# Expert layer of a two-block model: which weight slot an overflow tile uses, and in which order the weight loads are issued

## The reference, cut to what matters

```
# 32 experts, every token is sent to 2 of them: 512 (token, expert) rows
expert_id, weights = route(h)                # top-1 group of 8 experts, then top-2 inside it
ys[row] = (silu(x_row @ w_gate[e]) * (x_row @ w_up[e])) @ w_down[e]    # 2048 -> 256 -> 2048, float32
m[token] = sum over its two rows of weight * ys[row]
x = x + gate2 * m
```

## Time and profile before

| | |
|---|---|
| median of three runs | 2995.3 us |
| the profiled execution's own time | 2994.91 us |
| its span | 2993.1 us |
| mean granted TensorE clock | 0.89 of full |
| TensorE matmul busy | 2464.2 us (82%) |
| expert stage, first to last use of expert weights | 2343.4 to 2963.8 us of the span |
| bytes moved by DMA over the span | 610.12 MB |

### The profile page before, as it was taken

One profiled execution on the slowest core, in us unless ns is written; L12 is line 12 of the kernel. 1 busy time (PEld: TensorE's weight loads), 2 busy tenths in 40 slices (PEclk: granted clock), 3 DMA queues, 4 the chain that ended last, 5 costly groups with the idle time before them and its releaser, 6 DMA issues. The chain is left out here.

```text
span 2993.1 us, 42486 instructions
## 1 busy us (share of the span) xinstructions
PE 2464.2 (82%) x18072; PEld 1904.0 (64%) x18072; DVE 1146.7 (38%) x1421; ACT 810.1 (27%) x995; POOL 4.1 (0%) x8
## 2 busy tenths in 40 slices
PE   5997769977998898799999999959465767777774
PEld 5995549934786765699989989848334423333331
DVE  4752445544534301454554555544422211111112
ACT  3443223221113311444344344344201110111110
POOL 0000000000000000000000000000000000000000
PEclk8997889988977999899999999979786788899887
DMA  4447443565214510455555554334204597888886
GB/s 185 199 169 310 196 170 135 202 275 225 114 52 168 203 73 40 169 183 183 197 183 183 197 184 182 141 135 177 104 0 184 242 410 320 357 359 361 351 357 277
DMA packets 58490, 610.12 MB, mean 204 GB/s; under 512 B 5970, under 2 KB 6354, under 8 KB 13266
## 3 DMA queue, kind: packets, MB, share of 16 engines
q1 hardware_dynamic: 51410, 590.90, 49.9%
q10 hardware_dynamic: 6336, 12.58, 1.1%
q0 software_dynamic: 576, 4.19, 0.4%
HBM read 674.76 MB, written 14.68 MB: 230 GB/s over the span
## 5 line engine op out<-in xcount | busy, mean ns | idle before, releaser
L1883 DVE TENSOR_TENSOR ffn_w_lo<-ffn_raw,ffn_w_hi 128x2048 fp32r<-128x2048 f32 x128 | 293.1, 2291 | 234.5 <-ACT ffn_w_hi L1876 234.5
L2587 PE MATMUL psum<-moe_raw,moe_x_t 128*32 128x512 f32 x1536 | 240.0, 754 | 152.7 <-DMA moe_raw<-in_moe 151.2
L1876 ACT ACTIVATE ffn_w_hi<-ffn_raw 128x2048 fp32r<-128x2048 f32 x128 | 244.9, 1914 | 360.6 <-PE psum L1915 355.8
L1913 PE MATMUL psum<-u_hi,ffn_w_hi 128*128 128x256 f32 x1024 | 291.1, 284 | 15.1 <-DVE ffn_w_lo L1883 14.0
L1914 PE MATMUL psum<-u_lo,ffn_w_hi 128*128 128x256 f32 x1024 | 290.8, 284 | 0.0
L1915 PE MATMUL psum<-u_hi,ffn_w_lo 128*128 128x256 f32 x1024 | 290.8, 284 | 0.0
L2587 PEld LDWEIGHTS psum<-moe_raw,moe_x_t 128*32 128x32 f32 x1536 | 50.8, 126 | 273.9 <-issue 227.9
L1913 PEld LDWEIGHTS psum<-u_hi,ffn_w_hi 128*128 128x128 f32 x1024 | 197.7, 193 | 16.0 <-DVE ffn_w_lo L1883 14.2
L1913 PE MATMUL psum<-ffn_w_hi,ffn_hid_hi 128*128 128x512 f32 x512 | 199.4, 389 | 0.0
L1914 PE MATMUL psum<-ffn_w_lo,ffn_hid_hi 128*128 128x512 f32 x512 | 199.4, 389 | 0.0
L1915 PE MATMUL psum<-ffn_w_hi,ffn_hid_lo 128*128 128x512 f32 x512 | 199.2, 389 | 0.0
(11 more groups left out here) (538 smaller groups left out, 4492.2 us busy)
## 6 DMA issues: line engine op xcount, KB each, us to landing
moe_raw<-in_moe SPq DMA_DIRECT2D x144, 2048.0 KB
ring<-in_stream SPq DMA_DIRECT2D x107, 2048.0 KB, 10.9
ffn_raw<-in_ffn SPq DMA_DIRECT2D x128, 1024.0 KB, 4.8
expert_rows<-moe_stage ACTq DMA_DIRECT2D x48, 256.0 KB
x<-in_x SPq DMA_DIRECT2D x2, 1024.0 KB, 7.8
mem<-in_mem SPq DMA_DIRECT2D x2, 1024.0 KB, 15.0
out<-x SPq DMA_DIRECT2D x2, 1024.0 KB, 4.4
rw_ar<-in_lora SPq DMA_DIRECT2D x1, 1536.0 KB
```

Source lines behind the costliest of these rows:

```text
L1876: act.activation(self.w_hi[:, number % self.HIGHS], self.raw[:, number % self.RAWS], ACT.Copy)\
L1883: dve.tensor_tensor(self.w_lo[:, number % self.LOWS], self.raw[:, number % self.RAWS], self.w_hi[:, number % self.HIGHS].bitcast(F32), ALU ...
L1913: pe.matmul(out, lhs[0], rhs[0], start=start, stop=False)
L2587: mm = pe.matmul(summed(tile)[strip(q), :], e.x_t[:, tile // 4 % 2, UNIT_KC * u + c, strip(tile % 4)], w[:, c * COLS:(c + 1) * COLS], star ...
```

## The change: another slot for the overflow tiles, and another order of the loads

First tiles alone alternate: A always uses slot 0, B always slot 1. The overflow tile S uses slot 1, that of its predecessor B. `slot(n)` returns the slot and how many loads it has had by then. The loads are issued in the order A of the next triple, S of this triple, B of the next triple, each after the tile that used its slot last. TensorE's program is the same but for the slot and the count that it waits for.

```diff
+    @staticmethod
+    def slot(n):
+        i, part = n // 3, n % 3
+        return (0, i + 1) if part == 0 else (1, 2 * i + part)
+
     def load(self, sp, n, u):
-        sp.dma_start(self.raw[:, n % 2, u], self.weights[self.UNITS * Sorting.ORDER[n] + u]).then_inc(self.unit_in[n % 2][u], 16)
+        slot, _ = self.slot(n)
+        sp.dma_start(self.raw[:, slot, u], self.weights[self.UNITS * Sorting.ORDER[n] + u]).then_inc(self.unit_in[slot][u], 16)
...
-            for n in range(2, MOE_TILES):
-                spare = Sorting.ORDER[n] - EXPERTS
-                if spare >= 0:
-                    at = sp.value_load(sorting.spare_of[spare:spare + 1, 0:1], min_val=0, max_val=e.UNITS * (EXPERTS - 1))
-                    filled = sp.value_load(sorting.filled[spare:spare + 1, 0:1], min_val=0, max_val=1)
+            def free(n, u):
+                if u < 2:
+                    sp.wait_ge(e.used_up, 2 * n + u + 1)
+                else:
+                    sp.wait_ge(e.used_down, n + 1)
+            for i in range(MOE_SPARE):
+                spare = 3 * i + 2
+                if spare + 1 < MOE_TILES:
+                    for u in range(e.UNITS):
+                        free(spare - 2, u)
+                        e.load(sp, spare + 1, u)
+                at = sp.value_load(sorting.spare_of[i:i + 1, 0:1], min_val=0, max_val=e.UNITS * (EXPERTS - 1))
+                filled = sp.value_load(sorting.filled[i:i + 1, 0:1], min_val=0, max_val=1)
                 for u in range(e.UNITS):
-                    if u < 2:
-                        sp.wait_ge(e.used_up, 2 * (n - 2) + u + 1)
-                    else:
-                        sp.wait_ge(e.used_down, n - 1)
-                    if spare >= 0:
-                        e.load_spare(sp, n, u, at, filled)
-                    else:
-                        e.load(sp, n, u)
+                    free(spare - 1, u)
+                    e.load_spare(sp, spare, u, at, filled)
+                if spare + 2 < MOE_TILES:
+                    for u in range(e.UNITS):
+                        free(spare, u)
+                        e.load(sp, spare + 2, u)
...
             def up(tile, u):
-                pe.wait_ge(e.unit_in[tile % 2][u], 16 * (tile // 2 + 1))
-                w = e.raw[:, tile % 2, u]
+                slot, loads = e.slot(tile)
+                pe.wait_ge(e.unit_in[slot][u], 16 * loads)
+                w = e.raw[:, slot, u]
```

More of the change, by code:

```diff
@@ L2502, in __init__ @@
         self.raw = sb("moe_raw", [P, 2, self.UNITS, UNIT])
-        self.unit_in = [[sem(f"moe_unit_in{half}_{u}") for u in range(self.UNITS)] for half in range(2)]
+        self.unit_in = [[sem(f"moe_unit_in{slot}_{u}") for u in range(self.UNITS)] for slot in range(2)]
         self.used_up, self.used_down, self.parts = sem("moe_used_up"), sem("moe_used_down"), sem("moe_parts")
@@ L2515, in buffers @@
         self.hid, self.stage = sb("moe_hid", [P, 2, 2, ROWS]), sb("moe_stage", [P, self.STAGED, COLS])
+    @staticmethod
+    def slot(n):
+        i, part = n // 3, n % 3
+        return (0, i + 1) if part == 0 else (1, 2 * i + part)
     def load(self, sp, n, u):
-        sp.dma_start(self.raw[:, n % 2, u], self.weights[self.UNITS * Sorting.ORDER[n] + u]).then_inc(self.unit_in[n % 2][u], 16)
+        slot, _ = self.slot(n)
+        sp.dma_start(self.raw[:, slot, u], self.weights[self.UNITS * Sorting.ORDER[n] + u]).then_inc(self.unit_in[slot][u], 16)
     def load_spare(self, sp, n, u, at, filled):
+        slot, _ = self.slot(n)
         src = self.weights[bass.ds(at + u, 1)].rearrange("a p n -> (a p) n")
-        sp.dma_start(self.raw[:, n % 2, u], src, cond=filled).then_inc(self.unit_in[n % 2][u], 16)
+        sp.dma_start(self.raw[:, slot, u], src, cond=filled).then_inc(self.unit_in[slot][u], 16)
     def first_loads(self, sp):
@@ L2603, in down @@
                 pe.wait_ge(e.hid_done, tile + 1)
-                pe.wait_ge(e.unit_in[tile % 2][2], 16 * (tile // 2 + 1))
+                slot, loads = e.slot(tile)
+                pe.wait_ge(e.unit_in[slot][2], 16 * loads)
                 if tile >= 2:
                     pe.wait_ge(e.y_done, tile - 1)
-                w = e.raw[:, tile % 2, 2]
+                w = e.raw[:, slot, 2]
                 for c in range(2):
```

## The result

| | before | after |
|---|---|---|
| median (5 runs each, first comparison) | 2996.07 us | 3013.66 us (3008.65 to 3020.12) |
| ratio | | 1.0061, 95% interval 1.0044 to 1.0079 |
| profiled execution | 2994.91 us | 3010.95 us |
| span | 2993.1 us | 3009.1 us |

The change costs 17.6 us (13 to 24 by the interval); 21.6 us had been forecast. The chain of the page after names the stores beside the loads, 5% of the span; in that of before they are at 0%. Shares of the span by engine and by line, after; L2603 is up, L2627 down, L2593 and L2594 the gather.

A forecast was written before the change was run, and what follows sets the result against it. Four DMA engines that carry stores besides loads were taken as the bound. Unfilled triples 0, three holes less cover +22.6 us, the end -1 us: +21.6 us on 2994.9 us gives 3017 us, range 3000 to 3032.

The forecast's parts named there:

- The bound: Expert stage: the four DMA engines that run stores besides loads are 102% busy and set the pace; twelve have slack.
- Case 2: Rival: the 3.7 us pause in each of 13 unfilled triples is slack that prefetching closes; 2969 us, chance 0.09.
- Unfilled triples, value 0: In 13 of 16 triples, work on the four engines is conserved: still 37.7 us a triple, change 0.
- Case 4: Rival: in unfilled triples loads and stores run dry together, 2.5 us in each of 12; 3047 us, chance 0.07.
- The 14.4 us: Unfilled triples: time from B's unit 1 landing to the next B's release: up, gather, down twice and S.
- Filled triples: Three triples: the load queue empties after S's unit 1, three holes costing 22.6 us in all after store cover.
- The hole: Empty load queue after S's unit 1: release 5.8 us plus restart 1.7 to 3.9 us, taken as 8.6 us.
- The page's 2.0 us: Fixed cost of a DMA transfer by the skill's page, mostly completion; by it a hole is 7.8 us.
- The cover: Store work done inside the three holes, deducted from their cost: 0, 2.8 and 0.4 us, together 3.2 us.
- The end, -1 us: From 2958 to 2962 the four engines lose 1.4 us, which backed-up stores can use: -1 us taken.
- The sum: Whole kernel: +22.6 us for the holes and -1 us at the end, +21.6 us, giving 3017 us.
- Case 3: Rival: stores three deep do 8.4 us of work in each hole, so about no change; 2995 us, chance 0.06.

The follow-up runs named there:

- e5: Kernel before, with every store issued twice, the second copy to rows nobody reads: 3117.57 us, ratio 1.0419.
- e2: Kernel before, with each store issued as four DMAs of 32 partitions to use more engines: 2965.78 us, ratio 0.9908.
- e9: Kernel before's slots and order for the first four triples, the changed kernel's from n = 12 on: 2991.06 us, ratio 0.9988.
- e10: Changed kernel's slots and order for the first four triples, kernel before's from n = 12 on: 3020.86 us, ratio 1.0089.
- e8: Before's order for four triples, then changed slots with B's units 0, 1 ahead of S's unit 2; stores as four DMAs: 2911.66 us, 0.9735.

## Why the prediction was right

- **The bound.** Right. e5 shows it by adding load to four engines only, e2 by taking it off them. The trace before shows it directly: of the sixteen landings that make up a load, those of the B's unit 1 that is used at 2610.84 come by 2607.77 for twelve and at 2609.25, 2610.44, 2610.58 and 2610.80 for the last four. Case 2 (the pause is slack, 2969 us) falls.
- **Unfilled triples, value 0.** Right within what a comparison can tell: 37.8 us a triple for 37.7, and e9 lies between -0.28% and +0.04%. Stores did back up and take did wait, 154 us, without the four engines running dry: they were idle 0.1 us between 2520 and 2950 (0.4 us before), and the pauses became fewer and longer, as forecast. Case 4 falls. The 14.4 us from B's unit 1 to the next B's issue were too few, 18.4 us at least in this trace; with the four engines full nothing hung on it.
- **Filled triples.** Right in place, number and kind, and e10 puts all the cost there. Two sizes were off, in opposite ways.
  - The hole: I took 8.6 us, with bounds 7.5 and 9.7. From S's unit 1 to the use of its unit 2 it was 15.5, 15.8 and 15.9 us; less the 4.9 us of the unit itself, some 10.8 us, above my upper bound. In the first and third hole the release took 6.0 us and issue to use 9.5 and 9.9 us; the row of 9.5 us was the right one for them, and what the sum had wrong was to take 5.64 us off it, a unit with stores in turn, where the unit alone is 4.9 us, and then to take the middle with a restart of only 1.7 us. In the second the release ran at the lower clock (up 3.64 us) and took 8.3 us, and issue to use 7.6 us. The difference is the store: in the second hole it was all but done when the load began, and the load's sixteen landings came together (2446.19 to 2447.04); in the first it still ran, and the last four came at 2386.14 to 2387.41, behind twelve by 2385.63.
  - The page's 2.0 us, taken up in the prediction from the Trainium skill, "DMA: Bandwidth & Descriptors", section "Anatomy of one DMA", gave an estimated hole of 7.8 us, and the measured ones are longer. That section is on DMAs issued from GpSimd; these loads are issued by SP.
  - The cover: I allowed 3.2 us of stores under the three holes. The four engines were idle 18.3 us in them, so 32.5 - 18.3 = 14.2 us were not. 7.6 of these are stores alone in the empty queue, one in each hole (the windows above). The rest falls in the restart, where the load's first packets are slow (up to 1.75 us for one that takes 0.61 in flow) and the store's last ones run between them; I did not separate the two. I had argued that on even n the store comes after four spreads. In the first hole it is issued at 2375.88, ahead of three of them.
- **The end, -1 us.** Of the right size: from 2950 on the four engines were idle 2.5 us before and 1.0 us after.
- **The sum.** 21.6 us forecast, 22.0 in the profiled stage, 17.6 in the medians of the first comparison; e10, with the same filled stretch, 24.8, of which some is idle time elsewhere (30.1 us in all for 26.0). Of the 22.0, 16.5 are idle time of the four engines, where the sum had all of its 21.6, and 4.1 are longer packets (636.5 us of packets on each of them for 632.4), which the sum did not have: in the filled stretch a store packet of 2 KB takes 0.103 us in the mean for 0.084 before. 1.4 us are not placed. So the mechanism was right, but that the total came so near is in part luck: holes 6.7 us too short, cover 11 us too small, and 4.1 us of another kind.
- **Case 3** (holes covered by stores, 2995 us) had a point: cover was over four times what I allowed. But one store ran in each hole and not three, and the holes were longer too.

## What to carry to other kernels

Before calling a transfer-bound stage idle at a DMA share of 0.25, ask on how many engines (k of 16) the small transfers run: add the load queue's share to 16/k times that of the store queue and see whether it comes to 100%. When a buffer is given to the successor of the tile that still needs it, look for the last unit that is released only behind the successor's own earlier units: SP's queue runs dry there, whatever stands behind it. Prefetching earlier is worth nothing while a saturated engine sets the pace, and a good deal once it does not (e2 to e8: 54 us).

## What had not been expected of the hardware

- ScalarE's queue issued a store at 2375.88 while three activations that stand ahead of it in the program started only at 2376.23.
- Four DMAs of 32 partitions (64 KB each) were faster for the kernel than one of 128 (256 KB), by 29 us over 48 stores, although ScalarE's queue issues four for one, some 0.4 us each (2639.89 to 2641.18 in e2).
- A 2 MB load that takes 4.88 us in flow took 7.6 us from issue to first use onto an empty load queue, and 9.5 and 9.9 us where a store ran beside it.
- Runs of one kernel spread by up to 21 us (before on one chip: 2985.33 to 3006.02). The entry into the stage alone lies 16 us apart in the twelve traces, behind stages that are the same in all.
